# Sample states built by ScalarE and VectorE, prompt values turned by VectorE and through memory, in a one-core decoder layer

## The reference, cut to what matters

```
f = lb + (1 - lb) * sigmoid(f_raw);  k = 1 - f
S_new = diag(f) @ S + outer(k, v)
o     = S_new.T @ q
```

```
o_t = sum_s A[t, s] v_s;     S_end = sum_s (k_s decayed to the end) outer v_s
```

## Time and profile before

| | us |
|---|---|
| median of 3 runs | 1168.29 (1166.27 to 1168.39) |
| profiled execution, its own time | 1166.37 |
| its span, first to last instruction | 1164.6 |
| PE busy | 1153.4 |
| DVE busy | 1001.7 |
| ACT busy | 566.9 |
| POOL busy | 73.1 |

### The profile page before, as it was taken

One profiled execution on the slowest core, in us unless ns is written; L12 is line 12 of the kernel. 1 busy time (PEld: TensorE's weight loads), 2 busy tenths in 40 slices (PEclk: granted clock), 3 DMA queues, 4 the chain that ended last, 5 costly groups with the idle time before them and its releaser, 6 DMA issues.

```text
span 1164.6 us, 30898 instructions
## 1 busy us (share of the span) xinstructions
PE 1153.4 (99%) x12437; PEld 1034.2 (89%) x12437; DVE 1001.7 (86%) x1566; ACT 566.9 (49%) x819; POOL 73.1 (6%) x110
## 2 busy tenths in 40 slices
PE   9999999999999999999999999999999999999997
PEld 7888888888888899899998999989989999999886
DVE  6778799779867898998989989888898999998677
ACT  6545645654555644444444444444444444444544
POOL 2122320101000200000000000000000000000031
PEclk9999999999999999999999999999999999999999
DMA  7767876766566566666666666666666666667595
GB/s 255 240 198 208 237 212 195 233 193 196 182 207 199 181 217 198 196 194 204 216 197 195 193 208 213 194 196 193 213 195 204 215 202 198 204 209 230 175 230 150
DMA packets 199017, 238.07 MB, mean 204 GB/s; under 512 B 12805, under 2 KB 158664, under 8 KB 198672
## 3 DMA queue, kind: packets, MB, share of 16 engines
q1 hardware_dynamic: 192528, 222.13, 61.5%
q0 software_dynamic: 5056, 13.99, 4.2%
q10 hardware_dynamic: 1360, 0.92, 0.3%
HBM read 228.46 MB, written 9.01 MB: 204 GB/s over the span
## 4 chain that ended last, share of the span: by engine, by line
PE 91%; DVE 4%; DMA 2%; issue 1%; ACT 1%; SPq 0%; DVEq 0%; ACTq 0%
PE acc L2343 13%; PE acc L1958 10%; PE acc L1960 10%; PE acc L1962 10%; PE acc L2384 7%; PE acc L2346 6%; PE acc L2345 6%; PE acc L2324 6%; PE acc L2326 6%; PE wrk L2324 4%; PE wrk L2326 4%; PE acc L2387 2%; PE acc L2386 2%; DVE hl L994 2%; PE wrk L2115 1%
## 5 line engine op out<-in xcount | busy, mean ns | idle before, releaser
L994 DVE SCALAR_TENSOR_TENSOR hl<-raw,hl 128x1024 f16<-128x1024 f32 x414 | 493.5, 1219 | 55.4 <-ACT hl L631 52.5
L631 ACT ACTIVATE hl<-raw 128x1024 f16<-128x1024 f32 x414 | 420.7, 1052 | 166.9 <-DMA raw<-in_w_down_dram 91.7
L2343 PE MATMUL acc<-nrm,hl 128*128 128x264 f16 x1344 | 274.8, 276 | 0.0
L1960 PE MATMUL acc<-nrm,hl 128*128 128x264 f16 x920 | 253.9, 276 | 0.0
L1962 PE MATMUL acc<-nrm,hl 128*128 128x264 f16 x920 | 253.9, 276 | 0.0
L1958 PE MATMUL acc<-nrm,hl 128*128 128x264 f16 x920 | 253.9, 276 | 0.0
L2345 PE MATMUL acc<-nrm,hl 128*128 128x264 f16 x672 | 185.5, 276 | 0.0
L2346 PE MATMUL acc<-nrm,hl 128*128 128x264 f16 x672 | 185.5, 276 | 0.0
L2343 PEld LDWEIGHTS acc<-nrm,hl 128*128 128x128 f16 x1344 | 129.0, 98 | 17.8 <-DVE tg L1502 0.2
L2384 PE MATMUL acc<-big,hl 128*128 128x264 f16 x704 | 130.2, 276 | 0.0
L1958 PEld LDWEIGHTS acc<-nrm,hl 128*128 128x128 f16 x920 | 90.2, 98 | 13.3 <-issue 0.3
(11 more groups left out here) (491 smaller groups left out, 2246.7 us busy)
## 6 DMA issues: line engine op xcount, KB each, us to landing
raw<-in_w_gate_up_dram SPq DMA_DIRECT2D x168, 512.0 KB, 4.6
raw<-in_w_down_dram SPq DMA_DIRECT2D x88, 512.0 KB, 4.0
raw<-in_w_in_dram SPq DMA_DIRECT2D x80, 512.0 KB, 4.5
raw<-in_w_out_dram SPq DMA_DIRECT2D x32, 512.0 KB, 5.2
raw<-in_w_ple_gate_dram SPq DMA_DIRECT2D x32, 512.0 KB, 5.3
state<-in_state_hgrn_dram POOLq DMA_DIRECT2D x8, 512.0 KB, 6.9
out_new_hgrn_sample_dram<-state POOLq DMA_DIRECT2D x8, 512.0 KB, 5.2
raw<-in_w_gate_up_dram SPq DMA_DIRECT2D x16, 256.0 KB, 3.7
```

Of the source, the lines that this page charges most:

```text
L631: nc.scalar.activation(hi[:, st.hl_slot(j, half), :], raw[:, st.raw_slot(j), :], ACT.Copy, scale=WSCALE).then_inc(hi_done, 1)
L994: stt(lo[:, st.hl_slot(j, half), :], raw[:, st.raw_slot(j), :], WSCALE, hi[:, st.hl_slot(j, half), :], ALU.mult, ALU.subtract).then_inc(lo ...
L1960: mm(out, wh, x_lo[:, kt, :], start=False, stop=False)
L2343: mm(out, wh, n_hi[:, kt, :], start=jj == 0 and kk == 0, stop=False, skip_group_check=bool(up))
```

## The change

The sample states are no longer formed from outer products on PE. The values of four heads and 8 sequences are packed by DVE (`vs_pack`, 128x32), turned by one f32 transpose on PE (job `vs_c`, steps 26 and 51), copied by ACT to 32 rows, stored to memory by POOL (16 KB, `v_rows`), and loaded for each head with the same row on all 128 partitions (`rows_to_all`, 512 KB written, into one of two buffers `v_bc`). ACT scales the old state by f and the broadcast values by k, sequence by sequence (`sample_part`, 4 activations of 128x128 a part, 8 parts a pair), DVE adds the two (`new_states`, one sum of 128x1024 a head).

The prompt values are turned in 32x32 squares by one DVE transpose a quad (`turned_values`, steps 24 and 48), stored by POOL in four DMAs of 128-byte pieces (`values_out`), and loaded with tokens on the partitions (`values_in`) over `v_all`; ACT and DVE halve them from there at steps +13 and +15.

The steps of the last pair's halves and sums, of `oss`, the sample root and the sample mix move, and POOL clears the window margins after its last state store.

```diff
-SAMPLE_AT = (26, 38, 50, 58)
-BUF_AT, U_LAST_AT, OSS_AT = 44, (73, 80), 71
-RMS_AT, ROOT_AT, SAMPLE_ROOT_AT = 64, 65, 72
-O_NORM_AT, O_MIX_AT, SAMPLE_MIX_AT = (66, 67, 69, 71), (68, 70, 72, 74), 75
+PART_AT = ((28, 29, 30, 31, 32, 33, 34, 35), (40, 41, 42, 43, 44, 44, 45, 46),
+           (50, 51, 54, 54, 56, 56, 57, 58), (59, 60, 63, 64, 64, 65, 66, 66))
+ADD_AT = tuple((at[3] + 1, at[7] + 1) for at in PART_AT)
+S_HI_AT = ((36, 38), (46, 48), (59, 61), (67, 68))
+S_OUT_AT = (42, 52, 65, 72)
+ROWS_AT = (26, 51)
+BUF_AT, U_LAST_AT, OSS_AT = 44, (73, 80), 74
+RMS_AT, ROOT_AT, SAMPLE_ROOT_AT = 64, 65, 75
+O_NORM_AT, O_MIX_AT, SAMPLE_MIX_AT = (66, 67, 69, 71), (68, 70, 72, 74), 77
...
-X_FIRST = 27
+X_ROWS, X_FIRST, X_LAST = 16, 24, 28
+V_AT = (13, 15)
...
+            def values_out(c):
+
+                pool.wait_ge(vt_turned, c + 1)
+                for q in range(4):
+                    dst = vt_rows[c].rearrange("h (m i) (q f) -> q i (h m) f", i=32, f=32)[q]
+                    pool.dma_start(dst, vt_blk[32 * q:32 * q + 32]).then_inc(vt_out[c], 16)
+
+            def values_in(c):
+
+                pool.wait_ge(vt_out[c], 16 * 4)
+                for h in range(4):
+                    pool.dma_start(v_all[:, 4 * c + h, 0:SEQ].rearrange("p (a d) -> p a d", a=2),
+                                   vt_rows[c, h].rearrange("(a p) d -> p a d", a=2)).then_inc(vt_in[c], 16)
...
+            def rows_written(c):
+
+                pool.wait_ge(drained["act"], drain_of(f"vs_{c}")[1])
+                pool.dma_start(v_rows[c], vs_tok).then_inc(vs_out, 16)
+
+            def rows_to_all(h):
+
+                n = NSAMP * P
+                src = bass.AP(v_rows.tensor, v_rows.offset + h * n, [[0, P], [1, n]])
+                pool.dma_start(v_bc[h % 2].rearrange("p b v -> p (b v)"), src).then_inc(v_bc_in[h % 2], 16)
+
+            x_blocks(range(BUF_BEHIND, X_ROWS - 2))
+            values_out(0)
+            x_blocks(range(X_ROWS - 2, X_ROWS))
+            rows_written(0)
+            values_in(0)
+            x_blocks(range(X_ROWS, X_ROWS + 2))
+            pool.wait_ge(vs_out, 16)
+            rows_to_all(0)
+            rows_to_all(1)
+            x_blocks(range(X_ROWS + 2, X_FIRST))
             for p in range(PAIRS):
+                if p == 2:
+                    values_out(1)
+                    values_in(1)
+                    rows_written(1)
+                    pool.wait_ge(vs_out, 32)
+                    rows_to_all(4)
+                    rows_to_all(5)
                 for h in (2 * p, 2 * p + 1):
-                    pool.wait_ge(drained["dve"], drain_of(f"ou_{p}_3")[1])
+                    pool.wait_ge(state_new, h + 1)
                     pool.dma_start(io["new_hgrn_sample"][0, :, h, :, :].rearrange("b d v -> d b v"),
                                    state[:, h % 2, :, :]).then_inc(state_out[h % 2], 16)
+                    if p % 2 == 0:
+                        rows_to_all(h + 2)
...
+            for n in range(2):
+                last = nc.gpsimd.memset(win[n][:, :, 0:WPAD], 0.0)
+            last.then_inc(zero_ready, 1)
...
+                if r in V_AT:
+                    act.wait_ge(vt_in[c], 16 * 4)
+                    hs = slice(2 * V_AT.index(r), 2 * V_AT.index(r) + 2)
+                    nc.scalar.activation(v16[:, 0, hs], v_rows_of(c, hs), ACT.Copy, scale=TSCALE).then_inc(tok_hi, 1)
...
+            def sample_part(p, n):
+
+                old, h = n % 4 // 2 == p % 2, 2 * p + n // 4
+                x, gains = (state[:, h % 2], f_all) if old else (v_bc[h % 2], k_all)
+                if old:
+                    act.wait_ge(state_in[h % 2], 16 * (p + 1))
+                    act.wait_ge(acc_free, TPG * (3 * (p // 2) + 3))
+                else:
+                    act.wait_ge(v_bc_in[h % 2], 16 * (p + 1))
+                for b in range(4 * (n % 2), 4 * (n % 2) + 4):
+                    last = nc.scalar.activation(x[:, b, :], x[:, b, :], ACT.Copy, scale=gains[:, h, SEQ + b:SEQ + b + 1])
+                if n % 2:
+                    last.then_inc(state_kept if old else kv_ready, 1)
...
-            def pair_states(p, bs):
...
+            def new_states(h):
+
+                dve.wait_ge(state_kept, h + 1)
+                dve.wait_ge(kv_ready, h + 1)
+                tt(state[:, h % 2], state[:, h % 2], v_bc[h % 2], ALU.add).then_inc(state_new, 1)
...
+                nc.vector.tensor_copy(vs_pack.rearrange("p (h b) -> p h b", h=4), v_all[:, hs, SEQ:TOK]).then_inc(vs_packed, 1)
...
+            def turned_values(c):
+
+                if c:
+                    wait_job(f"sf_{c - 1}")
+                nc.vector.transpose(vt_blk, v_all[:, 4 * c:4 * c + 4, 0:SEQ]).then_inc(vt_turned, 1)
...
+            def sample_values(c):
+
+                pe.wait_ge(vs_packed, c + 1)
+                out = job(f"vs_{c}")
+                nc.tensor.transpose(out[0:4 * NSAMP, 0:P], vs_pack, ident[:]).then_inc(job_done, 1)
+                yield
```

## The result

The changed kernel takes 1190.8 us in the median of 4 runs (1188.1 to 1194.9), the kernel before 1168.0 beside it: 1.0204 times as long, 95% interval 1.0182 to 1.0226. Forecast were 1178.0 and a range up to 1183, so the time lies outside it. The direction was right and the place of the largest loss too; the size was not. The profiled execution of the changed kernel took 1188.1 us, its span 1186.3, which is 21.7 more than the span before.

A forecast was written before the change was run, and what follows sets the result against it. PE, busy 99% of the span, was taken as the bound, with DVE also near its limit. Terms -6.8 + 1 + 9.8 + 1.7 + 4.0 = +9.7 us gave 1176.1 profiled, 1178.0 as median; range 1162 to 1183.

The forecast's parts named there:

- PE's savings, -6.8: Projection: transposes and outer products removed from PE save 7.0 us, two new transposes cost 2 x 0.11; net -6.8 us.
- DVE's lead over PE stays; I cost it at nothing: Projection: DVE sheds about what PE sheds, so its lead stays, costed at zero; otherwise up to 2 us handed back.
- -17.1 us on DVE: DVE in the projection: eight sets of scaled sums from PSUM, 2.14 us each, go; with additions the net is -4.7.
- Block 32, +1 (0 to 2): First quad: the broadcast lands at 113.6, work ready at 115, PE there at 114.2; wait 1 us, bounds 0 and 2.
- Block 56, 9.8 (4 to 13): Third pair: POOL's serial chain through memory makes PE wait 9.8 us at block 56, bounds 4 and 13.
- -4.3: DVE before the third pair's chain: two sets of scaled sums go, putting DVE 4.3 us sooner at that place.
- Landings: DMA landing times from trace rows: stores 9.0 us from first issue, packed rows 4.3, broadcasts 5.8.
- Rival 3: Landings are short, as on SP's queue: block 56 waits 2.6 us, net -2.2, total 1166.1 us; chance 0.13.
- Clock, +1.7 once: After the long wait at block 56 PE's clock may fall once: half of 3.4, +1.7 us, bounds 0 and 3.4.
- ACT's copies, 21 us: ACT in the projection: 128 scaled 128x128 copies at 0.16 us start to start, 21 us in 32 parts; ACT has room.
- The end, +4.0 (0 to 6): Blocks 64 to 80: block 72 2.4 us later, small matmuls 0.9, sample mix 0.7; sum +4.0, bounds 0 and 6.
- the main term: Block 56: state load, stores, value loads, rows and broadcast in series on POOL delay ACT and PE; 9.8 us.

The follow-up runs named there:

- experiments 12 and 15: 12: samples' way alone (prompt values turned by PE), waits moved behind the evictions, 1167.1 us; 15: the same with the first windows moved later, 1167.8 us.
- Experiment 3: The changed kernel with the prompt values turned by PE as before, so the samples' way alone: 1175.6 us, 1.0066 times the kernel before.
- experiment 4: The changed kernel with each ACT part as one 128x512 activation at constant scale 0.5, gains left out: 1182.3 us, 1.0127 times the kernel before.
- experiment 7: The kernel before with only the end moves (last pair's halves and output, samples' sums, root and mix): 1168.0 us, 1.0003 times the kernel before.
- experiments 1 and 9: Both on the changed kernel. 1: POOL stores values before state 5's load, rows before value loads, 1181.9 us; 9: ACT's memory waits behind evictions, 1177.6 us.

## Why the prediction was wrong in size

The sum had +9.7 us, the ledger has 22.2. Of the 12.5 between them, 3.7 are at block 32, 2.7 at block 51, 3.2 at block 56 (clock included) and 2.9 at the end.

- **PE's savings, -6.8**: held. Outside the places of loss the changed kernel's stream is 7.0 us shorter, and with the samples' way alone (1.8 + 3.4 - 0.2 of the sum) and most waits off, PE is 5.0 us ahead at block 63 (experiments 12 and 15). (32 times 0.06 is 1.9, not 1.8, and 108 + 5.8 at block 32 is 113.8, not 113.6; neither matters.)
- **"DVE's lead over PE stays; I cost it at nothing"**: this step failed first. The -17.1 us on DVE were counted as if they could be spent anywhere. The scaled sums of the second pair stood at 148.80 and 155.57 in the kernel before, and at their place DVE now waits for PE:

```profile
155.57 2.14 DVE L1204 SCALAR_TENSOR_TENSOR state<-state,big,wrk 128x128 f32<-128x128 f32 x8
```

```profile
151.94 1.22 DVE L1318 TENSOR_TENSOR big<-big 128x1024 f32<-128x1024 f32 x1 [0.96 <-PE wrk L2135]
158.60 1.43 DVE L1254 TENSOR_TENSOR big<-big 128x256 f32<-128x256 f32 x4 [1.03 <-PE wrk L2150]
```

From 140 to 160 us DVE is busy 14.33 us (before 16.28), and it waits 1.08 more at 175.37, for ACT: much of what was saved was spent in waiting. What came in, a sum of 1.2, two subtractions (before, in steps 44 and 45) and a turn of 1.24, came in steps 46 to 49, where the kernel before had DVE busy 14.90 of 15.00 us from 170 to 185. The keys of block 51 were late: 2.7 us that the sum had at zero. Experiment 3, without the turn, waits 0.7 there instead of 2.3, experiment 4, with short copies on ACT, still 2.3; so the turn is most of it.
- **Block 32, +1 (0 to 2)**: 3.0, and 1.7 of lower clock, which I had allowed only once in the whole kernel. In this profile the landing was as forecast (6.0 us, forecast 5.8). The broadcast was issued at 109.05, where I had 108, since the four loads of 128 KB took POOL 2.91 us and not the 2.0 of loads half as large, and from ACT's first copy at 115.11 to PE's opening 2.3 us went by where 1.4 were forecast, the copies at half their price. In another profile of the same stretch the wait was 6.9, and there the landings were at fault: I took one value between bounds for a term that changes from run to run.
- **Block 56, 9.8 (4 to 13)**: 12.2, inside its bounds, but by two errors that offset each other. The chain was to start at 180.2 and started at 188.15, since the subtraction of head 3 ended 7.3 us later (186.26 + 1.22): 2.5 of PE's lead were not there after block 32, and of the "-4.3" of removed sums 2.0 had gone into waits for PE, and DVE then waited 1.1 for ACT. From there the chain went nearly as summed: to the loads 10.7 us (10.4 forecast, 9.27 of it to the landing of the stores, 9.0 forecast), 2.9 for them (2.0), 5.5 for the rows (4.3), 4.05 from issue to landing for the broadcast (5.8), 3.3 to PE's opening (2.1, where the copies were at half their price). PE itself was 7.3 us later at this place than forecast, by blocks 32 and 51. So the wait is 2.4 longer, and the 7.3 are in the time as well.
- **Landings**: the four kinds went by the trace's own rows. The rule of the Trainium skill (DMA: Bandwidth & Descriptors, Anatomy of one DMA) had the packed rows at an estimated 2.0 us and they took 5.2 and 6.1, the broadcasts at an estimated 3.2 and they took 7.0 in the median. It had the wait near 1 us; the trace decides against it. Rival 3, which had short landings too, falls: the broadcast of head 4 landed in 4.0 us (it had 4.5), but the stores took 9.27 (5.4) and the rows 5.2 (2.0).
- **Clock, +1.7 once**: 5.9 in three falls. It was at the lower level for 5.1 us after the long wait, and for 3.4 us behind two waits of 3.0 and 3.8 us.
- **ACT's copies, 21 us**: 40.2 us busy. The row I took (0.16 from start to start) was an eviction out of PSUM, with a constant scale; these read a scale from a column and SBUF. This is the mis-sized term with the largest measured price: in experiment 4 a part takes 0.62 us, about the 0.65 of the forecast, and the kernel 1182.3, 8.5 less and within the forecast's range. The ledger has no line of its own for it; what the profile of experiment 4 shows of it lies in blocks 56, 68 and 72.
- **The end, +4.0 (0 to 6)**: 6.9. The place was right and block 72 answers to it. The sum laid 2.4 on the two sums of states and 0.5 on ACT, and nothing on the moved halves, which experiment 7 bears out. The wait at block 68 (1.6) and the clock at 72 were missing.

As a whole: the mechanism named as the main term is shown (experiments 1 and 9 take it away by its two ends, order of the queue and order on ACT). That its wait of 12.2 us fell inside its bounds was luck, since the chain and PE both came over 7 us late. The sum failed in DVE's lead costed at nothing, in the copies at half their price and in a clock allowed to fall once, and because the waits were priced one at a time against a kernel that was otherwise on time. Each wait made the next engine later, and three of them brought the clock down.

## What to carry to other kernels

Work taken from an engine is worth something only until that engine's next idle row: look for the first wait after the place where it is removed, and count nothing beyond it; work added counts where it lands. Where engines execute in order, a wait for memory belongs behind the work that the bounding engine needs next, and a DMA that waits for something belongs behind those that are ready: here two lines of one queue were worth 8.9 us, and four step numbers 13.3. When two changes use one queue, try each alone and both: 0.7 and 8.4 us became 22.8.

## What the runs showed of the hardware that I had not expected

- A ScalarE copy of 128x128 f32 within SBUF lasts 298 ns with a constant scale and 390 with the scale read from a column; one copy of 128x512 with a constant scale lasts 621. Four small ones take 0.89 us with a constant scale and 1.26 with a column.
- A 16 KB DMA out of SBUF on POOL's queue landed after 5.2 and 6.1 us, while the 512 KB broadcast, which reads 4 KB for all partitions, landed in 4.0 to 8.3. With 32 times the bytes written the median went from 5.7 to 7.0.
- After a wait of 12.2 us PE's clock stayed at 1.2 GHz for 5.1 us of full work; after one of 3.0 us for 3.4. The 2.7 us at block 51 came with no fall in the changed kernel, but in experiment 1 that block took 7.9 us with the same wait of 2.3, so a fall can come or not after the same wait.
